# Grouped attention: projections, head norms and rotations in one block, with the queries' norm moved into the exponential's scale

## The reference

```python
def prep(h, use_rope):
    q, k, v = split(h @ w_qkv, [8 * 128, (8 + 2) * 128])
    q = rmsnorm_2(q.reshape(B, T, 8, 128), qk_g[0])     # x * rsqrt(mean(x*x) + eps) * g, per head
    k = rmsnorm_2(k.reshape(B, T, 2, 128), qk_g[1])
    v = v.reshape(B, T, 2, 128)
    if use_rope:
        q, k = rope2d(q, ang), rope2d(k, ang)           # rotation by axial angles
    return q.reshape(B, T, 2, 4, 128) * 128 ** -0.5, k, v

q_c, k_c, v_c = prep(h_ctx, False)
q_l, k_l, v_l = prep(h_lat, True)
k_all, v_all = concat([k_c, k_l]), concat([v_c, v_l])
y_lat = softmax(q_l @ k_all.T) @ v_all @ w_out          # four query heads share a key head
```

## Time and profile before

| | us |
|---|---|
| timed runs | 3735.37, 3739.18, 3740.56 |
| median | 3739.18 |
| span of the profiled execution | 3734.1 |
| TensorE busy in it | 3347.0 (90%) |
| VectorE busy | 2142.2 (57%) |
| ScalarE busy | 1444.4 (39%) |
| stage of the change, first query tile's end to first score | about 3302 to 3390 |

### The profile page before, as it was taken

The page is one execution under the profiler, slowest core; times in us unless marked ns, Lnnn a source line. Parts: engine busy times, 40 slices in busy tenths (PEclk is TensorE's granted clock), DMA queues, the critical chain, the costliest instruction groups (busy, mean ns, idle before and its releaser), DMA issues. The chain is left out here.

```text
span 3734.1 us, 53949 instructions
## 1 busy us (share of the span) xinstructions
PE 3347.0 (90%) x20396; PEld 2857.0 (77%) x20396; DVE 2142.2 (57%) x4090; ACT 1444.4 (39%) x2236; POOL 41.7 (1%) x66
## 2 busy tenths in 40 slices
PE   6987899999999788999999998899886999876897
PEld 4844899998888667999997887577545887664797
DVE  4522489875887513699767787334764332233453
ACT  3311444444555323444444554332234222232343
POOL 0000000000000000000000000000110000000000
PEclk8978999999999878999999999899988999988898
DMA  5465676556777524666567786323541332220353
GB/s 183 150 228 177 191 213 202 170 176 205 241 241 243 171 70 132 199 199 183 175 185 230 242 241 209 113 68 136 194 138 51 96 95 91 73 73 2 116 168 120
DMA packets 225063, 596.58 MB, mean 160 GB/s; under 512 B 27424, under 2 KB 97440, under 8 KB 224576
## 3 DMA queue, kind: packets, MB, share of 16 engines
q1 hardware_dynamic: 220656, 588.17, 50.4%
q10 hardware_dynamic: 4176, 5.29, 0.4%
HBM read 558.16 MB, written 35.19 MB: 159 GB/s over the span
## 5 line engine op out<-in xcount | busy, mean ns | idle before, releaser
L2287 PE MATMUL ps<-h_split,split_layer 128*128 128x256 f32 x6144 | 777.1, 286 | 9.3 <-DVE split_layer L2076 9.3
L2287 PEld LDWEIGHTS ps<-h_split,split_layer 128*128 128x128 f32 x6144 | 751.3, 193 | 11.8 <-DVE split_layer L2076 11.8
L2433 PE MATMUL ps<-split_layer,h_split 128*128 128x512 f32 x3072 | 700.3, 390 | 13.8 <-DVE h_split L2417 13.8
L2433 PEld LDWEIGHTS ps<-split_layer,h_split 128*128 128x128 f32 x3072 | 578.9, 189 | 134.7 <-DVE split_layer L2400 14.2
L750 PE MATMUL ps<-h_parts_ffn,split_ffn 128*128 128x512 f32 (+1 forms) x2112 | 382.9, 342 | 15.9 <-DVE split_ffn L716 8.5
L750 PEld LDWEIGHTS ps<-h_parts_ffn,split_ffn 128*128 128x128 f32 x2112 | 332.1, 193 | 67.3 <-issue 17.0
L2076 DVE TENSOR_TENSOR split_layer<-ring,split_layer 128x1024 fp32r<-128x1024 f32 x256 | 311.5, 1219 | 81.6 <-ACT split_layer L2215 80.0
L2400 DVE TENSOR_TENSOR split_layer<-ring,split_layer 128x1024 fp32r<-128x1024 f32 x256 | 313.6, 1225 | 0.1
L716 DVE TENSOR_TENSOR split_ffn<-ring,split_ffn 128x1024 fp32r<-128x1024 f32 x132 | 160.4, 1224 | 254.9 <-ACT split_ffn L694 246.9
L2223 ACT ACTIVATE kept_layer<-ps 128x256 f32<-128x256 f32 x256 | 98.4, 384 | 461.0 <-PE ps L2287 460.9
L2382 ACT ACTIVATE split_layer<-ring 128x1024 fp32r<-128x1024 f32 x256 | 267.6, 1045 | 4.5 <-PEq L458 4.5
(11 more groups left out here) (584 smaller groups left out, 3807.6 us busy)
## 6 DMA issues: line engine op xcount, KB each, us to landing
ring<-in_experts SPq DMA_DIRECT2D x512, 512.0 KB, 3.8
ring<-in_mod SPq DMA_DIRECT2D x96, 512.0 KB, 4.5
ring<-in_ada SPq DMA_DIRECT2D x96, 512.0 KB, 4.4
ring<-in_ffn_in SPq DMA_DIRECT2D x88, 512.0 KB, 3.6
hidden_layer<-kept_layer SPq DMA_DIRECT2D x256, 128.0 KB, 2.0
x_sb<-hidden_layer SPq DMA_DIRECT2D x256, 128.0 KB, 3.7
ring<-in_ffn_out SPq DMA_DIRECT2D x44, 512.0 KB, 3.7
ring<-in_peer_q SPq DMA_DIRECT2D x32, 512.0 KB, 3.7
```

The costliest lines, as they stand in the source:

```text
L2287: ins = nc.tensor.matmul(ps[:, 4 + j % 2, 0:T], w[:, part, c], self.hsplit[:, moving, k, :], start=(k == 0 and n == 0), stop=(k == KT - 1 ...
L2433: ins = nc.tensor.matmul(ps[:, 2 * t + h, :], wsplit(j, a)[:, t * P:(t + 1) * P], w[:, b, h * 512:(h + 1) * 512], start=(j == 0 and n == 0 ...
```

## The change

Five blocks behind the query projection (keys, values, head norms, two rotations) and the query projection itself become one block, `grouped_inputs`. In it:

- ScalarE copies a query tile out of PSUM and squares it from there too. TensorE counts (sums the squares of) head m-1 behind tile m, and multiplies the raw copy of head m-1 by a rotation matrix whose rows carry the queries' gain, which VectorE makes once (`turn_q`). VectorE finishes the rotation of head m-3 behind the low half of tile m.
- The queries are not multiplied by their inverse root any more. Roots of all heads are made at the end as columns, 128 tokens on the partitions (`q_rows`, once with plus and once with minus 128^-0.5). The attention multiplies the row maximum by the negative column, and the exponential takes the positive one as its scale per partition.
- The keys' counts, widening products and rotation stand between the value products.
- The copy of one column that started `project_parts` (L726) is gone.

The diff, cut to its core (signal bookkeeping at the end and unchanged context left out):

```diff
-    def attention(self, heads, n_keys, scale, scores, value, out, causal, hosted=0):
+    def attention(self, heads, n_keys, scale, scores, value, out, causal, hosted=0, rows=None):
...
-                        v.tensor_scalar(top[h % 2], top[h % 2], -scale, None, ALU.mult).then_inc(topped.sem, 1)
+                        if rows is None:
+                            v.tensor_scalar(top[h % 2], top[h % 2], -scale, None, ALU.mult).then_inc(topped.sem, 1)
+                        else:
+                            v.tensor_tensor(top[h % 2], top[h % 2], rows[:, 1, h * TT:(h + 1) * TT], ALU.mult
+                                            ).then_inc(topped.sem, 1)
                     if h >= 1:
                         g = h - 1
...
                             ins = s.activation(prob[h % 2][:, qt, 0:seen[qt]], score(h, qt), ACT.Exp,
-                                               bias=top[h % 2][:, qt:qt + 1], scale=scale,
+                                               bias=top[h % 2][:, qt:qt + 1],
+                                               scale=scale if rows is None else rows[:, 0, h * TT + qt:h * TT + qt + 1],
                                                accum_out=total[h % 2][:, qt:qt + 1])
...
+    def grouped_inputs(self, c, entry, q, k, vt, q_rows):
+        nc, ps, A = self.nc, self.ps, self.arena
+        v, s, mm = nc.vector, nc.scalar, nc.tensor.matmul
+        split, slots = self.split, self.split.shape[1]
+        mark = A.at
+        TK = TA // P
+        QN, KN = GQ_H * TT, GQ_KV * TK
+        q_sq, k_sq, shifted = A.take(2, T), A.take(GQ_KV, TA), A.take(2, T)
+        turn_q, rows = A.take(P), A.take(QN + KN)
+        cos, sin = c["axial"][:, 0, :], c["axial"][:, 1, :]
+        q_gain, k_gain = c["qk_g"][:, 0:1], c["qk_g"][:, 1:2]
+        used, free, done = self.unit_used, self.bank_free, self.dve_done
+        hi_done, mul_done, turn_made, q_turned, q_shifted = self.a, self.c, self.b, self.d, self.f
+        counted, inverted, rooted, diagonals, widened = self.summed, self.inverted, self.rooted, self.diagonals, self.widened
+        k_normed, k_turned = self.normalised, self.e
+        entry.finish()
+        u0, f0 = self.n_used, free.n
+        hi0, mul0, turned0, shifted0 = hi_done.n, mul_done.n, q_turned.n, q_shifted.n
+        at = {x: x.n for x in (turn_made, counted, inverted, rooted, diagonals, widened, k_normed, k_turned)}
+        N_M = GQ_H + 2 * GQ_KV
+        turned_to = lambda m: ps[:, 4 + m % 2, 0:T]
+        with self.block() as block:
+            @block.sync
+            def _(sp):
+                self.stream(sp, N_M)
+            @block.tensor
+            def _(pe):
+                def query_turn(m):
+                    pe.wait_ge(free.sem, f0 + m + 1)
+                    if m >= 2:
+                        pe.wait_ge(q_shifted.sem, shifted0 + m - 1)
+                    for t in range(TT):
+                        mm(ps[:, 7, m * TT + t:m * TT + t + 1], q_sq[:, m % 2, t * P:(t + 1) * P], self.ones[:, 0:1],
+                           start=True, stop=True)
+                    mm(turned_to(m), turn_q, q[:, m, :], start=True, stop=True).then_inc(q_turned.sem, 1)
+                def key_counts(g):
+                    pe.wait_ge(free.sem, f0 + GQ_H + g + 1)
+                    for t in range(TK):
+                        ins = mm(ps[:, 7, QN + g * TK + t:QN + g * TK + t + 1], k_sq[:, g, t * P:(t + 1) * P],
+                                 self.ones[:, 0:1], start=True, stop=True)
+                    if g == GQ_KV - 1:
+                        ins.then_inc(counted.sem, 1)
+                def key_widths():
+                    pe.wait_ge(diagonals.sem, at[diagonals] + 1)
+                    for g in range(GQ_KV):
+                        ins = mm(ps[:, 5 + g, :], self.ones, k_sq[:, g, :], start=True, stop=True)
+                    ins.then_inc(widened.sem, 1)
+                def key_turn():
+                    pe.wait_ge(k_normed.sem, at[k_normed] + 1)
+                    for g in range(GQ_KV):
+                        ins = mm(ps[:, 4, g * T:(g + 1) * T], c["rot"], k[:, g, LAT], start=True, stop=True)
+                    ins.then_inc(k_turned.sem, 1)
+                entry.tensor_norm(pe)
+                for m in range(GQ_H):
+                    pe.wait_ge(used.sem, u0 + m + 1)
+                    pe.wait_ge(free.sem, f0 + m + 1 - BANKS)
+                    w = split[:, m % slots]
+                    for kk in range(KT):
+                        col = slice(kk * P, (kk + 1) * P)
+                        if m == 0:
+                            entry.tensor_tile(pe, kk)
+                        for j, (a, b) in enumerate(((0, 0), (0, 1), (1, 0))):
+                            ins = mm(ps[:, m % BANKS, 0:T], w[:, a, col], self.hsplit[:, b, kk, :],
+                                     start=(kk == 0 and j == 0), stop=(kk == KT - 1 and j == 2))
+                    ins.then_inc(mul_done.sem, 1)
+                    if m == 1:
+                        pe.wait_ge(turn_made.sem, at[turn_made] + 1)
+                    if m:
+                        query_turn(m - 1)
+                for g in range(GQ_KV):
+                    m = GQ_H + g
+                    self.await_unit(pe, u0 + m)
+                    pe.wait_ge(free.sem, f0 + m + 1 - BANKS)
+                    for kk in range(KT):
+                        ins = mm(ps[:, m % BANKS, :], self.slot(u0 + m)[:, kk * P:(kk + 1) * P], self.hT[:, kk, :],
+                                 start=(kk == 0), stop=(kk == KT - 1))
+                    ins.then_inc(used.sem, 1)
+                    if g == 0:
+                        query_turn(GQ_H - 1)
+                    else:
+                        key_counts(g - 1)
+                for g in range(GQ_KV):
+                    m = GQ_H + GQ_KV + g
+                    self.await_unit(pe, u0 + m)
+                    pe.wait_ge(free.sem, f0 + m + 1 - BANKS)
+                    for t in range(TK):
+                        for kk in range(KT):
+                            ins = mm(ps[:, m % BANKS, t * P:(t + 1) * P], self.hT[:, kk, t * P:(t + 1) * P],
+                                     self.slot(u0 + m)[:, kk * P:(kk + 1) * P], start=(kk == 0), stop=(kk == KT - 1))
+                        if t == TK - 1:
+                            ins.then_inc(used.sem, 1)
+                        if g == 0 and t == 0:
+                            key_counts(GQ_KV - 1)
+                        if g == 0 and t == TK - 1:
+                            key_widths()
+                        if g == 1 and t == 1:
+                            key_turn()
+            @block.scalar
+            def _(act):
+                def high(m):
+                    self.await_unit(act, u0 + m)
+                    if m >= slots:
+                        act.wait_ge(mul_done.sem, mul0 + m + 1 - slots)
+                    s.activation(split[:, m % slots, 0, :], self.slot(u0 + m), ACT.Copy).then_inc(hi_done.sem, 1)
+                def query(m):
+                    act.wait_ge(mul_done.sem, mul0 + m + 1)
+                    if m >= 2:
+                        act.wait_ge(q_turned.sem, turned0 + m - 1)
+                    s.activation(q[:, m, :], ps[:, m % BANKS, 0:T], ACT.Copy)
+                    s.activation(q_sq[:, m % 2, :], ps[:, m % BANKS, 0:T], ACT.Square).then_inc(free.sem, 1)
+                entry.scalar_begin(act)
+                high(0)
+                entry.scalar_root(act)
+                entry.scalar_parts(act)
+                for m in range(1, GQ_H):
+                    high(m)
+                    query(m - 1)
+                query(GQ_H - 1)
+                for g in range(GQ_KV):
+                    m = GQ_H + g
+                    act.wait_ge(used.sem, u0 + m + 1)
+                    s.activation(k[:, g, :], ps[:, m % BANKS, :], ACT.Copy)
+                    s.activation(k_sq[:, g, :], ps[:, m % BANKS, :], ACT.Square).then_inc(free.sem, 1)
+                act.wait_ge(inverted.sem, at[inverted] + 1)
+                s.activation(rows, rows, ACT.Sqrt).then_inc(rooted.sem, 1)
+                for g in range(GQ_KV):
+                    m = GQ_H + GQ_KV + g
+                    act.wait_ge(used.sem, u0 + m + 1)
+                    s.activation(vt[:, :, g * P:(g + 1) * P], ps[:, m % BANKS, :].rearrange("p (a b) -> p a b", a=TK),
+                                 ACT.Copy).then_inc(free.sem, 1)
+            @block.vector
+            def _(dve):
+                def low(m):
+                    dve.wait_ge(hi_done.sem, hi0 + m + 1)
+                    v.tensor_tensor(split[:, m % slots, 1, :], self.slot(u0 + m), split[:, m % slots, 0, :].bitcast(F32),
+                                    ALU.subtract).then_inc(used.sem, 1)
+                def query_rope(m):
+                    dve.wait_ge(q_turned.sem, turned0 + m + 1)
+                    v.tensor_tensor(shifted[:, m % 2, :], turned_to(m), sin, ALU.mult
+                                    ).then_inc(q_shifted.sem, 1)
```

(56 more changed lines are left out.)

## The result

The median went from 3739.87 us (four runs) to 3712.24 (3708.82 to 3719.88, four runs): the ratio is 0.9928, 95% interval 0.991 to 0.9946, some 27 us. The forecast was 3711.6. A second measurement (the last experiment) gave a ratio of 0.9913 (0.9894 to 0.9931), some 32 us.

What follows compares the result with a forecast made beforehand. The stage was taken as bound by TensorE's own work and, in its holes, by VectorE and ScalarE. 24.1 + 3.8 - 0.3 = 27.6 us off 3734.1 gives 3706.5; plus 5.1, 3711.6 us, range 3702 to 3722.

Steps and rivals of the forecast that it cites:

- Stretch A: First instruction of query tile 1 to first score: 63.1 us with the entry's 0.2, against 87.18, so 24.1 less.
- A query's piece: Counts and rotation of one head between query tiles: 0.89 us of TensorE, 7.1 for eight heads.
- The keys' pieces: Keys' counts 1.7, widening 1.75 and rotation 0.92 us of TensorE between keys and values: together 4.4 us.
- the boundary: Last values tile with its copy and the block boundary, ahead of the first score: 1.15 us still open.
- The rivals of pace and of holes that stay: VectorE and ScalarE pace query tiles: 4.9 us, 3716.5, chance 0.10; moved pieces each wait: 19.2 us, 3730.8, chance 0.07.
- The clock inside the block: Merged block: full clock from tile 2 expected; rival has counts dropping it, 5.1 us, 3716.7 or 3720.5, chance 0.17.
- The entry: Ahead of query tile 1: one added 128x128 VectorE instruction before the first low half, on the path, costs 0.2 us.
- The exponential: In the attention: per-partition scale adds 0.08 us each; 4 of 16 count, 0.3 us lost, bounds none and 1.2.
- The attention's clock: First heads: full clock when scores begin saves 2.1 us on scores and 1.7 on head 0's values, together 3.8.
- B: First score to output projection, 58.66 us before; forecast 55.2 after 3.8 gained and 0.3 lost.
- The total: Whole kernel: net 27.6 us less, span 3734.1 to 3706.5, plus 5.1 from span to median: 3711.6 us, chance 0.62.

Runs made afterwards that it cites:

- the last experiment: Changed kernel measured again, unaltered (median 3710.48 us, ratio 0.9913 to the kernel before), beside one with unread products in the heads' and query tile 0's holes (3706.82, 0.9906).
- the tail experiment: Changed kernel with every moved query and key piece behind the last value product instead of between the tiles; median 3727.68 us, ratio 0.9972 to the kernel before.
- the fifth experiment: Kernel before, with five unread products in TensorE's hole of each head from head 1 on; 3735.66 us in one run, beside 3736.82 for the kernel before.

## Why the prediction was right, and where it was not

*Stretch A: right, by its own steps.* Forecast 62.9 us from tile 1, measured 63.33, 61.98 and, with four more squares, 63.2. A query's piece was put at 0.89 and took 3.72 - 2.91 = 0.81 (2.91 from 17.5 us for tiles 2 to 7 of the kernel before). The keys' pieces were put at 4.4 and took 2 x 0.81 + 1.72 + 0.87 = 4.2. No handoff holds TensorE up; the boundary, 1.15, took 0.99. Tile 1 gave some 0.9 us back (5.28 to its first count, against 4.4), since all of it ran at 1.2 GHz in that execution. So the sum held to 0.4 us in part because its errors offset each other: tile 1 took 0.9 more, the pieces 0.8 less. The rivals of pace and of holes that stay fall with the timeline. That the pieces must stand between other products was argued; the tail experiment shows that this is worth 9.3 us.

*The clock inside the block: right.* Counts, 0.36 us each time, do not bring it down: from tile 2 to the first score (3311.81 to 3368.77) it is 1.00, and no piece there is slowed. The tail experiment has the low clock behind its counts again, but there the holes came with them: the clock was 1.00 to the end of the keys' counts (3357.84 to 3359.60) and 0.56 in the widening products behind the hole of 2.29 (3361.97 to 3365.40). Which of the two did it is open.

*The entry:* 0.2 forecast, about 0.1 measured. *The exponential:* 0.08 us longer by the earlier trace rows, 0.088 by the profile (772 against 684 ns). The Trainium skill (ScalarE: Activation LUTs, "What ACT_TABLE_LOAD costs") says about 93 ns for a pointer operand; the measurement lies just below. Of the sixteen, the steps between later heads stayed 7.05 us, so there it is hidden. On the path it shows at the first head alone, where the hole ahead of the transposes is 2.58 and not 2.50 (2.50 too with the norm kept), so of the 0.3 us that I took some 0.1 are seen.

*The attention's clock: the step that failed.* "In the attention the clock should now be up when the scores begin" was right, and worth the 2.1 us that it said, but "together 3.8 us" was not: B lost 0.82. I took the drop in head 0's values for the last of the cold start. The fills show that it comes from the holes of 2.5 us in the heads themselves: three executions with the holes filled had no drop (B 54.88, 54.86, and 57.10 with cold first scores), all eight without had at least one (56.5 to 61.9). That later heads with the same holes run at 1.00 I had read as proof that holes of this size are harmless; it only shows that they do not always strike. In all eight the first of these drops comes behind the first or the second hole, between which TensorE works for 2.8 us at the full clock, where later heads have 4.5 us between two. The Trainium skill (TensorE: Matmul & The Clock Gate, "Why this matters for your kernels") warns of idle gaps between TensorE's bursts of work only where they are longer than these. The traces go further: behind holes of 2.5 us the clock fell to 0.50, and with fills that leave some 0.35 us of each it stayed up. Whether it is the hole or the small share of work around it that counts, no run here tells apart.

*The total.* The trace gives 22.5 us where the steps gave 27.6: 2.7 are missing in B (3.8 - 0.3 forecast, 0.8 measured), 2.0 in stages that did not change, 0.4 in A and the entry. The median still met the forecast (3739.87 - 3712.24 = 27.6 us less), and that is in part luck. I had added 5.1 us, the distance from the profiled span to the median. A span is 1.7 us below its run's time (3711.6 and 3713.32), so the other 3.4 only say that the execution profiled before was a short one; added to the forecast, they made up for most of what the steps promised too much. The fifth experiment shows where such an execution can be short: A, 87.17 in the profile before, took 90.29 there, and against that the change is worth 27.0 us in A alone. How often the kernel before runs one way or the other, two profiles do not tell.

## What to carry to other kernels

Where one engine's work runs through a chain of blocks, add up its instructions at the full clock, merge the blocks and lay the small dependent pieces between the long products. The sum held to half a microsecond here; the merged block with the norm's move took 14.5 us off the stretch, and the order of the pieces in it another 9.3. Read a low clock in a window as a question about the holes in that window, and not only about what came before it. Do not take one profile of the kernel before for its mean. And compare a forecast stage by stage: a median that fits can hide two errors.

## What was not expected of the hardware

Unread work on TensorE made stages shorter in the profiles. Five products in each hole of 2.5 us brought the heads from 57.8 to 59.9 us (four profiles of the changed attention) down to 54.9. One product in each hole of 0.2 to 0.4 us of tile 0 brought tile 1 from 5.49 or 4.49 us to 3.12, at 0.1 us for tile 0. The timed runs do not separate the kernel with both fills from the changed one.

TensorE's busy share in the trace does not tell its clock either. Tile 0 stayed at 0.50 and was busy for 8.0 of 10.8 us, the last counts of the kernel before were at 0.50 and busy for 3.0 of 3.0, and a later head ran at 1.00 and was busy for 4.54 of 7.05.
